# When GpSimd fetches the activations of the directly treated tiles: all during the second front, in chunks of 16

## The reference

```
q = (ht @ w_q).reshape(T, 8, 2, 128)
s = einsum('thpd,hpnd->thpn', q, sub_keys)        # 8 heads, 2 halves, 128 keys
s_top, i_top = top_k(s, 16)
cand = s_top[:, :, 0, :, None] + s_top[:, :, 1, None, :]
best_s, best_pos = top_k(cand..., 16)              # 16 experts of each head
experts, gates = ..., softmax(best_s)
a = gelu(einsum('td,tkd->tk', xt, u[e]))           # 128 experts per token
out = einsum('tk,tkd->td', g * a, v[e])
```

## Time and profile before

| | us |
|---|---|
| median of the runs | 2477.81 |
| lowest, highest | 2477.03, 2489.2 |
| span of the profiled execution | 2478.5 |
| PE busy | 2372.6 (96%) |
| DVE busy | 1798.1 (73%) |
| POOL busy | 1276.9 (52%) |
| 384 row fetches on POOL (L474) | 484.2 |
| 384 activation gathers on POOL (L479) | 485.7 |
| 112 lo parts on POOL (L470) | 303.7 |

### The profile page before, as it was taken

How to read it: one execution, slowest core, us unless ns; L and a number is a source line. 1 busy time by engine, 2 the same in 40 slices (tenths; PEclk the granted TensorE clock), 3 DMA queues, 4 the chain that set the end, 5 groups by cost and what they waited for, 6 DMA issues and landing times.

```text
span 2478.5 us, 34835 instructions
## 1 busy us (share of the span) xinstructions
PE 2372.6 (96%) x12777; PEld 2025.7 (82%) x12777; DVE 1798.1 (73%) x3382; ACT 1057.5 (43%) x1810; POOL 1276.9 (52%) x892
## 2 busy tenths in 40 slices
PE   7988999999999998999999999999999999999997
PEld 7768999999977766787787788788788788888886
DVE  4673696454367797659999778477587688888886
ACT  4443454554334322332333276366474333333333
POOL 0000599000352355547777756287374488888860
PEclk9987999999999999999999999999999999999999
DMA  4533677767764447556576678978988999999994
GB/s 160 162 128 100 221 223 220 262 216 231 245 195 133 158 143 260 197 193 193 179 221 196 193 237 282 319 244 292 337 288 277 329 336 357 340 349 349 346 365 159
DMA packets 252681, 596.86 MB, mean 241 GB/s; under 512 B 35792, under 2 KB 118224, under 8 KB 251872
## 3 DMA queue, kind: packets, MB, share of 16 engines
q1 hardware_dynamic: 182496, 385.69, 46.4%
q0 software_dynamic: 67712, 201.61, 25.0%
q10 hardware_dynamic: 2304, 7.34, 1.0%
HBM read 521.12 MB, written 73.40 MB: 240 GB/s over the span
## 4 chain that ended last, share of the span: by engine, by line
PE 35%; POOL 16%; DVE 5%; issue 4%; DMA 4%; ACT 2%; SPq 1%; DVEq 0%; ACTq 0%
PE ps L833 27%; POOL a_got L479 8%; POOL picked L474 7%; PE ps L863 3%; PE ps L1081 3%; DMA raw<-in_experts 2%; POOL sp_lo L470 1%; DMA picked<-in_experts,vidx 1%; DVE acc_odd L1568 1%; DVE acc L1568 1%; ACT sp_hi L697 1%; PE ps L879 0%; SPq L359 0%; DVE sp_lo L1617 0%; DMA v_raw<-in_experts 0%
## 5 line engine op out<-in xcount | busy, mean ns | idle before, releaser
L474 POOL DMA_INDIRECT picked<-in_experts,vidx x384 | 484.2, 1261 | 659.4 <-PE ps L833 219.6
L833 PE MATMUL ps<-ht_hi,sp_hi 128*128 128x256 f32 (+1 forms) x2048 | 703.0, 343 | 17.6 <-POOL sp_lo L470 14.4
L833 PE MATMUL ps<-ht_lo,sp_hi 128*128 128x256 f32 (+1 forms) x2048 | 691.8, 338 | 0.0
L833 PE MATMUL ps<-ht_hi,sp_lo 128*128 128x256 f32 (+1 forms) x2048 | 691.4, 338 | 0.0
L479 POOL DMA_INDIRECT a_got<-acts,aidx x384 | 485.7, 1265 | 121.7 <-issue 108.0
L470 POOL TENSOR_TENSOR sp_lo<-raw,sp_hi 128x1024 fp32r<-128x1024 f32 x112 | 303.7, 2726 | 358.8 <-ACT sp_hi L697 358.4
L833 PEld LDWEIGHTS ps<-ht_hi,sp_hi 128*128 128x128 f32 x2048 | 391.1, 191 | 60.7 <-POOL sp_lo L470 18.9
L833 PEld LDWEIGHTS ps<-ht_hi,sp_lo 128*128 128x128 f32 x2048 | 390.6, 191 | 41.4
L833 PEld LDWEIGHTS ps<-ht_lo,sp_hi 128*128 128x128 f32 x2048 | 391.3, 191 | 36.6
L1617 DVE TENSOR_TENSOR sp_lo<-raw,sp_hi 128x1024 fp32r<-128x1024 f32 x144 | 176.4, 1225 | 265.4 <-ACT sp_hi L697 265.0
L705 ACT ACTIVATE act_g<-ps 128x256 f32<-128x256 f32 (+1 forms) x256 | 125.8, 491 | 546.3 <-PE ps L833 546.0
(11 more groups left out here) (190 smaller groups left out, 3659.9 us busy)
## 6 DMA issues: line engine op xcount, KB each, us to landing
raw<-in_experts SPq DMA_DIRECT2D x256, 512.0 KB, 4.2
v_raw<-in_experts SPq DMA_DIRECT2D x128, 512.0 KB, 6.0
raw<-in_front SPq DMA_DIRECT2D x104, 512.0 KB, 3.8
acts<-act_g SPq DMA_DIRECT2D x128, 256.0 KB, 4.5
act_in<-acts SPq DMA_DIRECT2D x128, 192.0 KB, 6.0
acts<-act_g SPq DMA_DIRECT2D x128, 128.0 KB, 2.3
gates<-stage SPq DMA_DIRECT2D x16, 1024.0 KB, 8.9
g_in<-gates SPq DMA_DIRECT2D x128, 128.0 KB, 6.1
```

Of the source, the lines that this page charges most:

```text
L474: pool.indirect_dma_start(picked[n % SLOTS][:, :], None, v_rows, bass.IndirectOffsetOnAxis(ap=vidx[:, n // P, n % P:n % P + 1], axis=0)).t ...
L833: last = pe.matmul(out, l, r, start=start and k == 0, stop=stop and k == 2, skip_group_check=True)
```

## The change

`CHUNK` is 16, and each chunk has a semaphore of its own (24 in all). For tiles 0 and 1, `fetch` issues three activations for each visit behind a first chunk of 16, so that after visit 79 all 256 are issued, and none of these stands in the direct steps of tiles 2 to 5. For tile 2 the pattern is as before with the new chunk: 16 first, two for each of 16 visits, then one, so that they lead by 32.

```diff
-CHUNK = 8
+CHUNK = 16
...
-        a_in = [S[f"a_in{i}"] for i in range(4)]
+        a_in = [sem(f"a_in{i}") for i in range(VISITS // CHUNK)]
...
-                                        ).then_inc(a_in[n // CHUNK % 4], 16)
-
-            def fetch(n, first, end):
+                                        ).then_inc(a_in[n // CHUNK], 16)
+
+            def acts_front(k):
+                return CHUNK + 3 * k
+
+            def acts_last(k):
+                return CHUNK + k + min(k, CHUNK)
+
+            def fetch(n, first, end, acts):
 
                 k = n - first
-                for m in ((CHUNK + 2 * k, CHUNK + 2 * k + 1) if k < CHUNK else (k + 2 * CHUNK,)):
+                for m in range(acts(k), acts(k + 1)):
                     if first + m < end:
                         pick_act(first + m)
...
-                fetch(n, 0, 2 * P)
+                fetch(n, 0, 2 * P, acts_front)
...
-                fetch(n, 2 * P, VISITS)
+                fetch(n, 2 * P, VISITS, acts_last)
...
-                dve.wait_ge(a_in[c % 4], 16 * CHUNK * (c // 4 + 1))
+                dve.wait_ge(a_in[c], 16 * CHUNK)
```

More of the change, by code:

```diff
@@ L217, in encoder_program @@
             "a_done", "gelu_done", "w_ready", "w_hi_ready", "w_lo_ready", "y_done", "y_tile",
[L218 removed]
+            "sparse_ready", "acc_in0", "acc_in1", "acc_in2", "x2_in",
             "w_chunk", "visit", "combined", "y_added", "y_out", "late_in", "end_ss", "end_ms", "end_rms",
@@ L511, in _ @@
                     if mid < due:
-                        fetch(mid, 0, 2 * P)
+                        fetch(mid, 0, 2 * P, acts_front)
                         mid += 1
```

1 line of the change is left out of this document (removed).

## The result

The changed kernel takes 2561.68 us (median; 2561.2 to 2564.29), the kernel before 2477.42 in the same comparison. The ratio is 1.0322, with a 95% interval from 1.0291 to 1.0352: 3.2% slower. The forecast was 2529 us, so the sign was right and the time lies inside the range, but +51 us was foreseen and +84 came. The profiled execution has a span of 2559.7 us, 81.2 over the 2478.5 of the earlier trace rows.

A forecast was written before the change was run, and what follows sets the result against it. POOL's queue, not its busy sum, was taken to bind in the front's bursts, holding up DVE, then PE. 2478.5 + 66 - 17 - 6 + 8 = 2529.5, so about 2529 us, 2.1% slower; range 2495 to 2565.

The forecast's parts named there:

- A to D: Four bursts of second-front visits, 0–11, 29–44, 49–62, 63–84: rows forecast 11.0, 17.8, 16.3 and 33.8 us late.
- The front: +66 forecast: Second front: four POOL issues per visit make rows late; 7.7 + 17.8 + 16.3 + 23.7 us reach PE.
- row j's time, 7.6 + 5.25 (j - 5): Landing of a burst's row j: first visit 1.3 us, cycles of 5.25 us beyond five rows ahead, 6.3 us landing.
- the excess over the minimum, 2 x 0.14 = 0.28 us for a visit: POOL's front cycle: 0.28 us, from the front's mean, added to four least issues of 4.96, giving 5.25 us.
- The ends of 4.96 and 6.1: Range of POOL's four-issue cycle, in us: least cost and dense-stretch cost; front loss 55 or 101 us.
- The reserves: Slack hiding late rows: attention waits leave 7.7 of A's 11.0 us; chunk 50 covers 10.1 us in D.
- The rival of a partial reserve: DVE's reserve swallows A and D, only B and C count: +19 us, 2497 us; chance 0.16.
- The direct steps: -17 forecast: Tiles 2 to 5: without gathers between POOL's lo parts, PE's waits and lost clock go, -17 of 19 us.
- What is late next is the lo part itself (ready in time once the queue is short): Direct steps: behind the removed 2.83 us gather, POOL's lo part would be ready in time; taken for -17 us.
- The gate stage: -6 forecast: Visits 125 to 255: no gathers behind them, so PE's 5.7 us wait for the one-hot operand goes.
- Tile 2: +8 forecast: Tile 2's start: sixteen visits with two gathers make row 276 11.6 us late; +8 reaches PE.
- the rivals, for times beyond 2564: Heavier case: time exceeds 2564 us only if PE's pauses also cost clock in PE-paced stretches; chance 0.08.

The follow-up runs named there:

- experiment 1: The changed kernel with the gather pace of before in the front, chunks of 16 kept; 2483.45 us, ratio 1.0007.
- 6: Old-pace kernel with chunks of 16, early gathers placed outside the bursts, last stage's doubled gathers over eight visits; 2473.08 us, ratio 0.9957.
- 3: The changed kernel with chunks of 8 and two activation gathers per front visit instead of three; 2522.94 us, ratio 1.0151.
- experiment 12: The changed kernel with the long mask builds of tiles 2 to 5 left out (wrong choices, only direct steps read); 2544.62 us, ratio 1.0274.
- 2: The changed kernel with chunks of 8 instead of 16, three gathers per front visit kept; 2550.31 us, ratio 1.0259.
- 4: The changed kernel with chunks of 8, front near before's pace, no gathers behind the first two direct lo parts; 2529.95 us, ratio 1.0181.
- 7: The changed kernel with the masks' comparisons as scalar_tensor_tensor instead of tensor_tensor; 2559.59 us, ratio 1.03.
- 8: The spread placement of 6 with the masks' comparisons as scalar_tensor_tensor; 2473.2 us, ratio 0.9962.
- 9: The changed kernel with each visit's row fetch issued ahead of its gathers; 2558.05 us, ratio 1.0316.
- 11: The spread placement of 6 with chunks of 8 and the last stage as in before; 2476.82 us, ratio 0.9987.
- 5: Experiment 1 with the last stage's doubled gathers over eight visits instead of sixteen; 2476.12 us, ratio 0.9977.

## Why the prediction was right, and where it was off

**The mechanism stood.** POOL's queue binds in the bursts, DVE waits for rows, PE for what is behind the visits. DVE's waits for rows in A to D were put at some 90 us and are 115. PE's last product of the query weights was put 55 to 75 us later; it starts at 1166.2 instead of 1090.6, 75.6 later. Of the signs named one failed: PE still waits for POOL's lo parts in the direct steps. The loss is 0 where the pace is undone (experiment 1) or placed outside the bursts (6), and grows with the issues per visit as the model says (3). That the range held is partly luck. Its upper end, 3 us above the measured time, was set for a cycle of 6.1 us and -15 us in the other stages; the cycles were 5.46 to 5.82, and the other stages came to +5.6.

**The front: +66 forecast, +75.6 measured.** The term is row j's time, 7.6 + 5.25 (j - 5). Both its numbers were off. Counted from a burst's first visit, the first row fetch starts 1.5 us behind the first visit and the last visit 5.0 us behind its row's issue: 6.5, not 7.6, since the landing was taken from the median of the whole kernel (6.3 us) and is shorter here. The cycle is (59.7 - 1.5)/10 = 5.82 us in B (59.7 is where the fetch of its last row starts), (46.4 - 1.5)/8 = 5.61 in C and (88.9 - 1.5)/16 = 5.46 in D, not 5.25. With these B is 6.5 + 58.2 - 42.3 = 22.4 late, C 6.5 + 44.9 - 33.3 = 18.1, and row 84 6.5 + 87.4 - 57.8 = 36.1: the measured 22.4, 18.2 and 36.0. The step that failed is "the excess over the minimum, 2 x 0.14 = 0.28 us for a visit": it took a mean over the whole front, quiet stretches included. In a burst bound by POOL the excess is 0.5 to 0.9, 0.5 of it on the row fetch that coincides with the visit. The ends of 4.96 and 6.1 held it. The longer cycle cost 5.7 + 2.9 + 3.4 = 12 us, and the shorter landing gave back 1.1 in each of B, C and D; 1.1 between B and C had no term.

The reserves were read well. In A 7.7 of 9.8 us remain behind the attention's waits (7.7 of 11.0 were forecast), and D covers 36.0 - 26.2 = 9.8 us, where the difference of two rows had given 10.1. The rival of a partial reserve needed three times that.

The Trainium skill ("SBUF — State Buffer", section "Who interferes with whom") infers that a tensor_tensor with both inputs in SBUF leaves descriptor generation alone. The trace of after speaks against it once more: the fetch at 1224.77 took 2.82 us beside DVE's two mask products, and 0.95 at the same place of the order in experiment 12, where these are short. The fetches also take their row numbers from a tile (`vidx`), and no run tells whether this reading or the descriptors are held up.

**The direct steps: -17 forecast, -3.6 measured.** This is the step that failed outright: "What is late next is the lo part itself (ready in time once the queue is short)". It isn't ready. The 2.83 us gather of the earlier trace rows was a sign of what DVE did at that moment, and I took it for the cause. With the gather gone, the row fetch stands in its place beside the mask build and takes 2.82 us. And the lo part ahead of both now stands still itself. Before, it won against the same comparison, which took 4.47 us (POOL, then DVE):

```profile
1142.18 2.61 POOL L470 TENSOR_TENSOR sp_lo<-raw,sp_hi 128x1024 fp32r<-128x1024 f32 x1
```

```profile
1142.47 4.47 DVE L1478 TENSOR_TENSOR one<-paf,iota 128x2048 f32<-128x2048 f32 x1
```

After, it is the lo part that takes 6.95 us and the comparison 2.29, though the one starts 0.26 us ahead of the other and started 0.29 us ahead before. In all eight kernels without gathers here the longest lo part is 6.95 us, in the four profiles with one gather for a visit it is 3.9 to 4.5; why it turns isn't shown. Of PE's 11.5 us 6.7 stay, 4.4 of them behind this lo part, and 3.1 come in for DVE's choices. The eight kernels without gathers here (changed, 2, 4, 6 to 9, 11) take 317.9 to 319.0 us, against 322.0 to 322.3 in three profiles with one gather (before twice, 5). Experiment 1, with one gather, took 319.6, a case between that I can't explain: its third mask build stands the other way round to POOL's lo part (the first comparison takes 4.47 us, in 5, with the same order, the second), and its fourth begins 4.0 us earlier than in 5. Without the masks the -17 is there and more: 302.7 us, -19.3. The prediction's price of these waits, 11.5 us and 7.5 for the clock, was thus near, and what would take them away was wrong.

**The gate stage: -6 forecast, -3.1 measured, not confirmed.** Two profiles of before differ by 5.9 us there. All changed kernels but 4 take 477.7 to 481.8 us, also 1, 5, 6 and 11, which still issue one gather per visit in this stage. So the absence of gathers isn't the cause that I named. Common to them is that gathers are further ahead of their use; which of it helps, if anything beyond scatter does, stays open.

**Tile 2: +8 forecast, +12 measured.** By experiments 1 and 5, equal but for the doubled gathers, these cost 9.0 us (110.6 against 101.6). The other 3 can be scatter: the first profile of before was the shortest, 98.9 us, where the other kernels with its last stage take 99.7 to 102.6. The mechanism and the +8 stand, as PE's idle time (8.1 us). The sum gave no price to the clock that these pauses cost: PE is busy for 4.0 us longer than in the first profile of before, and 2.5 longer in experiment 1 than in 5. The prediction had named this cost among the rivals, for times beyond 2564.

**The sum.** Front +9.6, direct steps +13.4, gate stage +2.9 and tile 2 +4.3 above the forecast: every miss went the same way, and together they are the 30 us between 51 and 81. The 23 of the first two are traced to their steps; of the other 7 the runs show only that they are within what two profiles of before differ by, stage for stage.

## What to carry to other kernels

A queue that just keeps pace has no room for early work, however idle its engine is by sum: find the bursts of its consumers, count issues per consumer in them, and put prefetches between the bursts, where 27 more gathers (45 with those beside the first two lo parts) cost nothing here, while 151 spread evenly cost 76 us. When a long instruction stands in front of a stall, ask what the other engines do at that moment before taking it for the cause; removing it may put its successor in the same spot. When two totals agree, compare them part by part before calling it a repeat. Before a term of a few us is read out of a stage, see how much that stage differs between profiles of the same order of instructions.

## What the runs showed of the hardware

DVE's operations with two long inputs (128x2048) and POOL's two-input lo part exclude one another nearly fully, in either form of the instruction. POOL's 2.4 us became 6.95 beside 4.5 us of comparisons, and elsewhere DVE's comparison took 4.47 us instead of 2.29 while a lo part of 2.77 ran. So one of the two stands still while the other works, and which one varies: the lo part began 0.29 us ahead of the comparison and went through (2.61, the comparison 4.47), and began 0.26 us ahead and stood still (6.95, the comparison 2.29). Beside a visit's scalar_tensor_tensor of 128x1024 a lo part took 2.6 us for 2.4 in a few cases (experiment 12 at 1224.02), and an indirect fetch 0.5 more (1.44 for 0.94, the mean of burst B). An indirect fetch that meets no such operation is constant to 0.01 us (0.94 or 0.95, with 0.30 between two), and each further one in a cycle costs just about that: cycles of three issues took 4.20 to 4.54 us and cycles of four 5.46 to 5.82.
